# Conv-group sums and scaling moved from GpSimd to VectorE, split copies halved, a shorter end, in a two-layer hybrid backbone

## What is computed

```python
for l in range(DEPTH):                                   # DEPTH = 2
    h = modulate(rmsnorm(x, g_mix[l]), sh1, sc1)
    q, k, v, u = split_in(h @ w_in[l])                   # one projection for both groups
    a_out = latent_attention(rope_2d(q), rope_2d(k), v, k_ctx, v_ctx, attn_sink[l])
    z = u[..., :512] * sigmoid(u[..., 512:])             # the convolution group
    z = depthwise_conv31(z) + b_dw
    mu = mean(z); var = mean(square(z - mu))             # layernorm of the group
    cv_out = silu((z - mu) * rsqrt(var + EPS) * ln_g + ln_b)
    x = x + gt1 * (concat(rmsnorm(a_out, g_a), rmsnorm(cv_out, g_c)) @ w_o)
    h2 = modulate(rmsnorm(x, g_ffn[l]), sh2, sc2)
    x = x + gt2 * swiglu(h2, w_gate_up[l], w_down[l])
    # layer 0 does the same for the context tokens; layer 1 needs only their keys and values
return rmsnorm(x, g_final)
```

## Time and profile before

| | us |
|---|---|
| median of 3 runs (lowest, highest) | 1572.58 (1570.73, 1575.07) |
| the profiled execution, whole time | 1575.53 |
| its span, first to last instruction | 1573.7 |
| TensorE busy | 1518.1 (96% of the span) |
| VectorE busy | 924.8 (59%) |
| ScalarE busy | 537.8 (34%) |
| GpSimd busy | 128.4 (8%) |
| mean granted clock of TensorE, share of full | 0.991 |

### The profile page before, as it was taken

How to read it: one execution, slowest core, us unless ns; L and a number is a source line. 1 busy time by engine, 2 the same in 40 slices (tenths; PEclk the granted TensorE clock), 3 DMA queues, 4 the chain that set the end, 5 groups by cost and what they waited for, 6 DMA issues and landing times.

```text
span 1573.7 us, 22653 instructions
## 1 busy us (share of the span) xinstructions
PE 1518.1 (96%) x8802; PEld 1227.2 (78%) x8802; DVE 924.8 (59%) x1511; ACT 537.8 (34%) x866; POOL 128.4 (8%) x163
## 2 busy tenths in 40 slices
PE   5999998999999999999999999998999999999996
PEld 2865774588888888888888889776579788888885
DVE  2683789777666425675853466678877533333335
ACT  3312368724322112222122243147845322222222
POOL 0033121040000000000000000620020000000000
PEclk9999999999999999999999999999999999999998
DMA  8672510013333123333332123510022233333322
GB/s 345 224 222 80 208 47 20 9 41 121 107 120 120 54 93 110 144 120 134 147 107 67 50 71 103 157 52 3 28 65 84 90 96 94 94 100 99 94 90 84
DMA packets 39865, 161.16 MB, mean 102 GB/s; under 512 B 5616, under 2 KB 6000, under 8 KB 33648
## 3 DMA queue, kind: packets, MB, share of 16 engines
q1 hardware_dynamic: 35856, 148.72, 28.0%
q0 software_dynamic: 3936, 11.45, 2.7%
HBM read 149.76 MB, written 2.10 MB: 96 GB/s over the span
## 4 chain that ended last, share of the span: by engine, by line
PE 88%; DVE 6%; ACT 2%; issue 2%; DMA 1%; SPq 0%; DVEq 0%; ACTq 0%
PE banks L514 74%; PE banks L543 3%; PE banks L655 2%; PE banks L667 2%; PE banks L682 2%; PE banks L451 2%; PE banks L719 1%; DVE row_max L1214 1%; PE banks L501 1%; PE banks L483 1%; DMA ada_first<-in_w_ada 1%; DVE prob L1237 1%; ACT prob L868 1%; DVE ada_sum_context L1181 0%; ACT w_high L785 0%
## 5 line engine op out<-in xcount | busy, mean ns | idle before, releaser
L785 ACT ACTIVATE w_high<-raw 128x1024 fp32r<-128x1024 f32 (+1 forms) x178 | 185.4, 1041 | 721.3 <-PE banks L514 708.1
L1097 DVE TENSOR_TENSOR w_low<-raw,w_high 128x1024 fp32r<-128x1024 f32 (+1 forms) x178 | 216.7, 1217 | 233.6 <-ACT w_high L785 230.1
L514 PE MATMUL banks<-h_high,w_high 128*128 128x512 f32 (+1 forms) x1248 | 310.7, 330 | 3.0 <-DVE tmp L1142 1.1
L514 PE MATMUL banks<-h_high,w_low 128*128 128x512 f32 (+1 forms) x1248 | 304.8, 325 | 0.0
L514 PE MATMUL banks<-h_low,w_high 128*128 128x512 f32 (+1 forms) x1248 | 303.8, 325 | 0.0
L514 PEld LDWEIGHTS banks<-h_high,w_high 128*128 128x128 f32 x1248 | 193.4, 189 | 38.1 <-issue 17.0
L514 PEld LDWEIGHTS banks<-h_low,w_high 128*128 128x128 f32 x1248 | 193.5, 189 | 20.9
L514 PEld LDWEIGHTS banks<-h_high,w_low 128*128 128x128 f32 x1248 | 192.1, 189 | 20.5
L1141 DVE COPY shift_product<-banks 128x2 f32<-128x2 f32 x78 | 12.4, 158 | 200.5 <-PE banks L514 189.9
L514 PE MATMUL banks<-h_normal_high,w_high 128*128 128x512 f32 x304 | 119.1, 392 | 2.7 <-DVE h_normal_low L1497 2.7
L514 PE MATMUL banks<-h_normal_low,w_high 128*128 128x512 f32 x304 | 119.0, 391 | 0.0
(11 more groups left out here) (192 smaller groups left out, 2203.0 us busy)
## 6 DMA issues: line engine op xcount, KB each, us to landing
raw<-in_w_gu SPq DMA_DIRECT2D x88, 512.0 KB, 3.5
ada_raw<-in_w_ada SPq DMA_DIRECT2D x21, 1024.0 KB, 5.7
raw<-in_w_dn SPq DMA_DIRECT2D x32, 512.0 KB, 3.5
raw<-in_w_mix SPq DMA_DIRECT2D x28, 512.0 KB, 5.1
ada_in_ff<-in_w_ada SPq DMA_DIRECT2D x12, 1024.0 KB, 5.6
raw<-in_w_out SPq DMA_DIRECT2D x16, 512.0 KB, 3.5
ada_first<-in_w_ada SPq DMA_DIRECT2D x7, 1024.0 KB, 15.1
raw<-in_w_dn SPq DMA_DIRECT2D x16, 384.0 KB, 3.0
```

What stands on the lines that cost most here:

```text
L514: last = mm(bank[:, 2 * slot + bk, 0:b - a], weights[w][:, k0_w + k, :], rhs[:, k0_rhs + k, a:b], start=(k == 0 and n == 0), stop=(k == kt ...
L785: f(wH[j][:, 0:k, :], raw[j][:, 0:k, :], ACT.Copy).then_inc(w_high, 1)
L1097: tt(wL[j][:, 0:k, :], raw[j][:, 0:k, :], f32(wH[j][:, 0:k, :]), ALU.subtract).then_inc(w_low, 1)
```

## The change

- GpSimd no longer adds the squared deviations, scales the deviations, or adds the squares of the convolution output. VectorE does these. The three additions of squared deviations stand in `qkv` at t = 1 behind the split of the weights. The four multiplications (`scale_deviation`) stand at t = 3, in layer 1 before the split of the weights and in layer 0 behind `q_low`, and read the broadcast straight from PSUM; ScalarE's copy of it to `sq[1]` is gone. The additions of the later squares stand in attention turns 15, 18 and 19. GpSimd still adds the four conv tiles for the mean and the residual in `ob`.
- In attention the two weight blocks are split in halves of 128x512: ScalarE in turns 9 to 12, VectorE in turns 12, 13, 14 and 16. Squares move to turns 13, 14, 16 and 17, `conv_high` to 18 to 21, `conv_low` to 22 to 25.
- In the first gate-up stage of layer 1 the remaining tiles 3 to 7 are all made in the second pair, and their low parts in the third.
- At the end, the eighth square is not added to `ssum`: TensorE makes the token means of `ssum` (seven squares) and of the eighth square and adds them in PSUM. There is no mark. Ten small products whose result nobody reads (`keep_busy`, 4 + 2 + 4) are put between these steps. ScalarE takes one root of a dummy before the last `dn` stage, so that its table is loaded there.

```diff
             def conv_norm(layer, n, width):
-                if n in (20, 21):
-                    split_high(layer, "qkv", 2, n - 20)
+                if n in (9, 10, 11, 12):
+                    split_high(layer, "qkv", 2, (n - 9) // 2, (n - 9) % 2)
...
-                elif n in (9, 10, 11, 12):
-                    k = n - 9
+                elif n in (13, 14, 16, 17):
+                    k = (13, 14, 16, 17).index(n)
...
+            def scale_deviation(layer, width):
+
+                dve.wait_ge(bc_ok, stat_index[layer, "var"] + 1)
+                for k in range(CT):
+                    tt(z[:, k, 0:width], z[:, k, 0:width], wide[:, 512 * BC:512 * BC + width], ALU.mult).then_inc(ln_y, 1)
...
                     rope_product(layer, t, context or t == 0)
+                    if t == 3 and not context:
+                        scale_deviation(layer, width)
                     split_low(layer, "qkv", t // 2, t % 2)
+                    if t == 1:
+                        dve.wait_ge(dev_ok, CT * layer + 2)
+                        chain.link(tt(ssum[:, 0:width], cv[:, 0, 0:width], cv[:, 1, 0:width], ALU.add))
...
+                        tt(ssum[:, 0:width], ssum[:, 0:width], cv[:, 3, 0:width], ALU.add).then_inc(conv_sum, 1)
                     if t > 1:
                         q_low(layer, t - 1, width)
+                    if t == 3 and context:
+                        scale_deviation(layer, width)
...
-                            normal_product(*((0, 3), (3, 6), (6, 8))[i])
-                        if plain:
-                            normal_low(6, 8)
+                            normal_product(*((0, 3), (3, DT), (DT, DT))[i])
...
-                pool.wait_ge(rs_ok, rs_index[layer, "var"] + 1)
-                for k in range(CT):
-                    nc.gpsimd.tensor_tensor(z[:, k, 0:w], z[:, k, 0:w], sq[1][:, 0:w], ALU.mult).then_inc(ln_y, 1)
```

## The result

The changed kernel takes 1560.19 us (median of 4 runs, 1559.14 to 1561.37), the kernel before 1571.65 in the runs made with it (4 runs, 1570.55 to 1575.07). The ratio is 0.9921, with a 95% interval of 0.9906 to 0.9935, so 11.5 us are saved. The forecast was 1560.6. The profiled execution took 1561.37 us, its span 1559.6, at a mean granted clock of 0.997 (before: 1575.53, 1573.7 and 0.991).

A forecast was written before the change was run, and what follows sets the result against it. The prediction took TensorE's work, waits and half-clock stretches as the bound. Its terms 0 - 4.2 - 3.7 - 4.4 + 0.3 = -12.0 us, applied to the median 1572.58, gave 1560.6 us, range 1555.5 to 1567.0 for 8 in 10.

The forecast's parts named there:

- Layer 1's `qkv`: Before layer 1's attention: scores start 1.8 us earlier and 2.4 us of half clock come back, -4.2 us.
- The 1.9 us at the broadcast: Layer 1's qkv: TensorE's 1.22 us wait at the broadcast grows by 0.65 because VectorE's line 1308 ends later.
- Attention: Both layers: stalls removed against VectorE work added, -1.2 us, plus 2.5 us of half clock back in layer 0, -3.7 us.
- the cost of VectorE's new work: Both attentions: additions, marks and half splits add 5.8 us to VectorE, not hidden in full because the engines are nearly full.
- VectorE's 7 us of stalls: Both attentions: GpSimd's additions cost VectorE some 7 us, which the change removes.
- Gate-up: Layer 1's gate-up: 2.7 us of wait for the normalised low part and 1.7 us of half clock go, -4.4 us.
- Both slacks: Layer 1's gate-up: w_low and the later split block each come 0.3 us before TensorE wants them.
- The end: After the last product: small products lengthen TensorE's path, the full-clock broadcast takes 1.0 instead of 2.08, +0.3 us.
- The clock drops again: Rival, chance 0.20: a wait moves, so half-clock gains in layer 1 or layer 0 don't come; 1564.3 us.
- VectorE bounds attention: Rival, chance 0.13: VectorE's added work in turns 12 to 25 makes attention +2 instead of -3.7; 1566.3 us.
- The stalls aren't GpSimd's: Rival, chance 0.04: long VectorE instructions have another cause and stay, so nothing pays for added work; +5.1, 1577.7 us.
- the clock stays up: Layer 1's qkv: with waits of about 0.7 and 1.9 us the clock stays full, giving back 2.4 us.

The follow-up runs named there:

- e1: Kernel before, with only the remainders of the normalised activations (tiles 6 and 7) made in the second gate-up pair; 1567.94 us, ratio 0.9971.
- e4: Kernel before, with only the new end (token means in two parts, ten small products, early table load); 1572.46 us, ratio 0.9998.
- e9: Changed kernel, with VectorE's three additions of squares in each layer's attention cut to one column; 1559.62 us.
- e10: Changed kernel, with the two weight splits in attention whole again instead of halved; 1560.53 us.
- e8: Changed kernel, with the old distribution of the normalisation behind the third gate-up pair; 1562.58 us, ratio 0.9929.
- e2: Kernel before, with only the additions of squared deviations and the scaling moved from GpSimd to VectorE; 1568.55 us, ratio 0.9973.
- e5: Changed kernel, with GpSimd adding two tables into unread data at its old ten places in each layer; 1566.05 us, ratio 0.9952.
- e7: Changed kernel without the first keep_busy(4) at the end; 1558.93 us, ratio 0.9906.
- e6: Changed kernel, with GpSimd making two one-table copies for each unread two-table addition at its old ten places; 1562.50 us, ratio 0.9930.
- e3: Kernel before, with only attention changed (additions of later squares on VectorE, halved splits, new places); 1569.17 us, ratio 0.9971.
- e11: Changed kernel run again with nothing edited; 1559.15 us, ratio 0.9919 to the kernel before.

## Why the prediction came out right, and where its steps did not

The total was right, 1560.6 against 1560.19, but by luck: two errors in it cancelled. From the profile of before (span 1573.7) to the second profile of the changed kernel (1557.5) the four parts of the forecast came to -14.5 us, not -12.0. The whole span is 16.2 us shorter; 1.3 of the rest lie before attention begins, where the first weights came 0.7 us sooner.

**Layer 1's `qkv`, -4.2 forecast.** Measured -1.93 to the scores (22.45 to 20.52) and -2.32 behind them (10.43 to 8.11), -4.25. The part in front of the scores is the change's: the wait became 0.63 as forecast (0.7). The part behind them is the clock's, and the step that ties it to the wait is only half borne out: `e1` and `e4` keep the wait of 3.16 us and have 8.11 there too, so the profile of before had caught a stretch that need not come with the wait. The 1.9 us at the broadcast came as 0.67 for `w_low` and 1.21 at the broadcast: the later end of VectorE's line reached TensorE one step earlier, in the product ahead. The working also counts a shuffle that "stalled a little"; the 512-column shuffle there takes 0.74 us before and 0.74 after, so that term (0.2 us) was nothing.

**Attention, -3.7 forecast.** Measured -4.2 in layer 0 and -1.45 in layer 1: -5.65. The term that failed is the cost of VectorE's new work, taken one for one at 5.8 us and half hidden in the middle value. The additions, 4.0 of the 5.8, cost almost nothing: `e9` gives back 0.1. The price of GpSimd's stalls without the clock is at most 1.45 in layer 1, of which 0.34 go to the halved splits if `e10` is right. In layer 0, 3.4 us less at half clock made 1.2 us (89.65 to 88.45 in `e1`), so the 6.8 us cost about 2.4 by this estimate, near the 2.5 forecast, and the stalls the other 1.8. So of VectorE's 7 us of stalls, about 3 were on the path, by this estimate.

**Gate-up, -4.4 forecast.** Measured 331.15 - 326.57 = -4.58. `e8` splits it: 3.0 for the wait and what follows directly; `e4` and `e8` against before (329.6 to 331.15) give 1.55 for the stretch. Here too the stretch doesn't follow from the wait each time (`e4`, `e8`). Both slacks, forecast as 0.3 us, held: the first `w_low` was ready at 1216.33 + 1.23 = 1217.56, for a product that started at 1218.00, the second at 1222.67, for one at 1223.44, and the one wait for `w_low` in the list is that in `qkv`.

```profile
1216.33 1.23 DVE L1113 TENSOR_TENSOR w_low<-raw,w_high 128x1024 fp32r<-128x1024 f32 x1 [1.07 <-ACT w_high L798]
```

**The end, +0.3 forecast.** Measured -0.05. The terms of the working add up to 1563.0 for the second means, not 1562.8, so it should have said +0.5. Fillers are cheaper than 0.5 us each (4 in 1.7 us), and a broadcast at full clock takes 1.02 as forecast.

**What cancelled.** The forecast subtracted its sum from the median of the runs, although 6.6 us of the sum were a clock that only some runs lose. The -16.2 hold for a profiled execution at a clock of 0.991. That execution (1575.53) lies 3.9 us above the median of 1571.65, and the second profile of the changed kernel (1559.32) 0.9 below that of 1560.19: 16.2 - 3.9 - 0.9 = 11.4, which is what the medians show. In 49 runs of the kernel before, made beside the experiments on three chips, the mean clock and the time go together:

| mean granted clock | runs of before | median us |
|---|---|---|
| 0.991 | 20 | 1574.6 |
| 0.992 | 6 | 1572.8 |
| 0.993 | 7 | 1572.8 |
| 0.994 | 9 | 1570.2 |
| 0.995 | 6 | 1568.8 |

(one more lay at 0.987 and 1579.4). The changed kernel has 0.997 to 0.999 in all of its 10 runs. Not all of that difference is time: the mean takes in the end, where the clock falls as TensorE waits and then has no more to do, and the fillers put that off. The end of before stood at half clock for 11.7 us of its last 15, that of the changed kernel for 5.5 of its last 12.5, which is 0.002 of the mean. `e4`, with the new end alone, has runs at a mean clock of 0.995 that take 1572.3 to 1573.6 us, where before takes 1568.8. So a mean clock can be compared only between kernels with the same end.

So the gain at the median is smaller than from the profile: attention gave 2 us more than forecast, and the clock at the median gave less than the 6.6 us counted. The step to mend is to treat a stretch at half clock as something with a frequency.

**The rivals.** "The clock drops again" did happen, behind layer 1's broadcast, in 4 of the 10 profiles that have the new order there (e2, e5, e7, e10) and in none of the 4 with the old one, but at 0.8 us, not at the 2.4 that the prediction gave it: it had priced the stretch as if it fell on the scores. The changed kernel's own two profiles don't have it, but with the same order in the other four, "the clock stays up" was no safe step. "VectorE bounds attention" is refuted by `e9`. "The stalls aren't GpSimd's" is refuted by `e5`.

## To carry to other kernels

Before moving small work to GpSimd, look for VectorE instructions that are long only while GpSimd runs: a two-input instruction there can cost more on VectorE than doing the work on VectorE would, above all if VectorE has gaps (here 4.0 us of additions cost 0.1; a 768-column addition takes VectorE 0.95 us, and the same one on GpSimd had stalled it by up to 1.6). Price a half-clock stretch by its frequency over several executions, not by the one profile, and take a removed wait at its own length first. Fillers that keep TensorE awake belong only where it would otherwise wait; on its own path they cost their full time.

## What the runs showed of the hardware

- **A stall of VectorE beside GpSimd lasts until GpSimd's instruction ends.** The six one-element additions of `e5` that took over 0.3 us each ended 0.01 to 0.03 us after an instruction of GpSimd, and so did the five long ones of `e6` and the three of the kernel before. The longest took 0.69 us beside two-input additions of 256 columns (0.73 when nothing held them up), 0.35 beside copies of 256 columns (0.40), and 1.78 beside a two-input addition of 768 columns that took 1.92, against 0.15 alone. Instructions that read PSUM for one input, reductions from PSUM, shuffles and the reciprocal kept their times.
- **Half-clock stretches come and go behind identical waits.** Behind the wait of 3.2 us before the scores the clock fell in 2 of 4 profiled kernels, and in none of the 10 without it; behind the 2.7 us for `h_normal_low` in 3 of 5, and in none of the 9 without it. Around turn 14 of layer 0 it fell in all 4 kernels that had GpSimd's sums there, and in none of the 9 others that had neither them nor `e5`'s two-input additions (`e5` had 3.4 us at 263.2). So the first goes with GpSimd's sums, and the waits make the two others possible without bringing them each time; what decides in which execution they come is open, since no run here varied the work ahead of them.
- **A half-clock stretch can come where TensorE is busy throughout.** In the first profile of the changed kernel TensorE was busy for all of the 3.4 us at 308.2, in `e3` for all of the 10.2 us at 305.6. Ahead of 308.2 stood waits of 0.63 and 0.53 us and twelve one-column products in 1.4 us. The same waits and products stand in `e11` and in the kernel before, at full clock.
- **The clock explains the scatter.** Between 0.991 and 0.995 the time of before differs by 5.8 us, 1.4 to 1.5 for each 0.001.
